# HGRN mixer, first head pair: decay tables in PSUM in place of SBUF

## Chip, cores and metric

One Trainium2 chip, one of its cores. The metric is the device time of one execution in microseconds (us). The kernel before takes 2683.29 us, the median of 3 runs (2683.0 to 2686.62).

## What is computed

The reference is a hybrid encoder trunk of two layers over 512 tokens of width 1024, in fp32. The first layer's mixer joins an HGRN2 gated linear recurrence (4 heads of 128x128 state, in both directions) and a Mamba-2 mixer; a dense SwiGLU follows. The second layer has an S5 mixer and an expert SwiGLU. The change concerns the HGRN2 part only:

```python
def _hgrn2_one_direction(q, k, v, logf):
    ...
    bc = jnp.cumsum(chunks(logf), axis=3)
    ...
        diff = bi[:, :, :, None, :] - bi[:, :, None, :, :]
        decay = _masked_exp(mask, diff)
        scores = jnp.einsum('bhtsd,bhsd->bhts', decay * qi[:, :, :, None, :], ki)
        o = (jnp.einsum('bhts,bhsv->bhtv', scores, vi)
             + jnp.einsum('bhtd,bhdv->bhtv', qi * jnp.exp(bi), state))
    ...
```

The score of query t against key s is the sum over d of q[t,d] k[s,d] exp(b[t,d] - b[s,d]), with b the running sum of the log forget gates. The backward direction is the same on the flipped sequence.

## The kernel before

It is one program with an instruction list for each engine, written by hand, and semaphores between them. The order on an engine is the order of the code; no scheduler moves anything.

The scores of a head are built over 9 levels. At level l the 512 tokens fall into blocks of 2·2^l; the queries of one half of each block meet the keys of the other half. A boundary between the halves splits the decay into a factor for the query and one for the key, so a level is an elementwise scaling of q and k and a product of the two on TensorE. Heads go in pairs: `unit(u)` gives (head, level, side) for u = 0 to 35, and units 0 to 17 (PAIR_UNITS is 18) are the first pair, two heads by turns, level 0 to 8. For one unit:

- ScalarE (L2128 to L2149) writes two decay tables of 128x512 into a buffer of the unit: B, the exponential of the prefix sums (L2144), and A, that of the suffix sums (L2146). At level 0 A is a copy of k (L2148). The buffers A_ and B_ are three of each in SBUF, taken by turns (u % 3). Before unit u ScalarE waits, from u = 3 on, until TensorE has read unit u-3 (s_gram, L2140), and from level 1 on until GpSimd has updated the sums for this level and head (s_upd, L2143), which is its work of unit u-2.
- GpSimd (L1059 to L1079) waits for ScalarE's unit u (s_exp), then brings both sums of this head to the next level: "near" (L1076) adds the block edges to the suffix sums and "far" (L1079) to the prefix sums, both 128x512 in SBUF, in place. It does so for all units of a pair but the last two. Ahead of it stand a memset (L1060) and the sums of the two key tables, `ksum` (L1064, two instructions).
- VectorE (L2792 to L2813) waits for s_exp and multiplies in place: B by q (L2798) and, from level 1 on, A by k (L2801). Then it takes the scores of unit u-2 out of PSUM (`scores`: L2710 for the diagonal at level 0, L2723 to copy by a mask up to level 6, L2726 and L2729 above).
- TensorE (L1461 to L1490) waits for the two products (s_X), then multiplies A and B into one of PSUM's banks 0 to 2, taken by turns, which VectorE must have emptied. Each such bank use is a slot, numbered 0 to 21 in a pair. Between slots stand fills (`dense_fill`, L1434 to L1438): pieces of the input projections that don't depend on HGRN2, accumulated in banks 6 and 7 and taken out by ScalarE (L2122). `fills_after_slot` says how many have been done after a slot, 29·(v+1)/22 rounded down in the first pair, so one or two after each slot. One fill is two matmul records of 128x512.

```python
a_at, prefix, suffix = ab_at + 2 * T * (u % 3), lf_at + T * hd, rs_at + 2 * T * side
if l:
    act.wait_ge(s_upd, updates_before(hd, l))
act.activation(by_halves(a_at + T + hs, -hs, hs), by_halves(prefix + hs, D_STEP - hs, hs), ACT.Exp)
```

After the last unit of the first pair TensorE computes the outputs of its two heads (`hg_out`, L1407) into banks 3 and 4. Banks 3, 4 and 5 hold nothing else while the units of the first pair run; in the second pair the normalisation of the first pair's outputs uses them. SyncE moves tables of the S5 layer between DRAM buffers meanwhile (L916, L920), and then loads further projection weights when fills have used the old ones (L955).

Of the kernel before, what the change touches and what calls it, by code (L numbers as in the profile page):

```python
# [10 lines left out]
ALU = mybir.AluOpType  # L11
ACT = mybir.ActivationFunctionType
AX_X = mybir.AxisListType.X

P = 128
# [38 lines left out]
def build_program(nc, I, out):  # L54
    x, p_in = I["x"], I["p"]
    _, T, D = x.shape
# [25 lines left out]
    with ctx:  # L82
        def sem(name):
            return ctx.enter_context(nc.semaphore(name))
# [15 lines left out]
        psum = ctx.enter_context(nc.psum_tensor("psum", [P, 8, 512], F32))  # L100
# [126 lines left out]
        s_X = sem("scaled_qk_ready")  # L227
        s_upd = sem("prefix_updated")
        s_gram = sem("gram_done")
# [119 lines left out]
        qT = hga.take(4 * T).rearrange(v4, a=4)  # L349
# [17 lines left out]
        q_at, k_at, lf_at, D_STEP = base, base + 4 * T, base + 20 * T, 4 * T  # L367

        UNITS, SIDES = HEADS * LEVELS, 2
        PAIR_UNITS, PAIR_SLOTS = 2 * LEVELS, 2 * (LEVELS + 2)  # L370

        def unit(u):

            pair, l, side = u // PAIR_UNITS, u % PAIR_UNITS // 2, u % 2
            return 2 * pair + side, l, side
# [4 lines left out]
        def first_slot(u):  # L380
            hd, l, side = unit(u)
            return PAIR_SLOTS * (hd // 2) + (2 * side + 1 if l == 0 else 2 + 2 * l + (side if l < LEVELS - 1 else 2 * side))

        def last_slot(u):
            return first_slot(u) + (unit(u)[1] == LEVELS - 1)

        def out_unit(hd):
            return PAIR_UNITS * (hd // 2 + 1) - 2 + hd % 2

        def updates_before(hd, l):  # L390

            return 2 * (LEVELS - 1) * (hd // 2) + 2 * (l - 1) + hd % 2 + 1

        def blocks_of(hs):
            return [[2 * hs, T // (2 * hs)], [1, hs]] if hs > 1 else [[2, T // 2]]

        def by_halves(at, step, hs):

            return bass.AP(sbuf, at, [[words, P], [step, 2]] + blocks_of(hs))
# [810 lines left out]
        def _(pe):  # L1210
# [191 lines left out]
            def hg_out(hd):  # L1402
                pe.wait_ge(s_gdr, last_slot(out_unit(hd)) + 1)
                if hd >= 2:
                    pe.wait_ge(s_mix, hd - 1)
                for c in range(TC):
                    m = pe.matmul(psum[:, 3 + hd % 2, :], vtok[:, c, hd * P:(hd + 1) * P], S_main[hd % 2][:, c, :],  # L1407
                                  start=c == 0, stop=c == TC - 1)
                m.then_inc(s_o, 1)
# [542 lines left out]
        def _(act):  # L1952
# [154 lines left out]
            def hg_square(hd):  # L2107
                act.wait_ge(s_o, hd + 1)
                act.activation(mixT[:, hd, :], psum[:, 3 + hd % 2, :], ACT.Square).then_inc(s_osq, 1)

            def hg_rms(hd):
                act.wait_ge(s_oss, hd + 1)
                act.activation(mixT[:, hd, :], psum[:, 5, :], ACT.Sqrt, bias=eps, scale=1.0 / P).then_inc(s_orms, 1)

            def fill_drain(i):
                name, b = DENSE[i]
                act.wait_ge(s_grp, 4 * gidx[name] + b + 1)
                if (name, b) == ("xs", 0):
                    act.wait_ge(s_X, PAIR_UNITS)
                    act.wait_ge(s_upd, 2 * (LEVELS - 1))  # L2120
                out_ = zs[:, b, :] if name == "z" else raw[b + 4 * (name == "bc")]
                act.activation(out_, psum[:, 6 + i % 2, :], ACT.Copy).then_inc(s_drA, 1)  # L2122
# [6 lines left out]
            for u in range(UNITS):  # L2129
                hd, l, side = unit(u)  # L2130
                hs = 1 << l
                for i in range(len(DENSE)):
                    if i != DT_BLOCK and unit_after[i] + 3 == u:
                        fill_drain(i)
                if u in (PAIR_UNITS + 3, PAIR_UNITS + 4):
                    hg_square(u - PAIR_UNITS - 3)
                if u in (PAIR_UNITS + 6, PAIR_UNITS + 10):
                    hg_rms((u - PAIR_UNITS - 6) // 4)
                if u >= 3:
                    act.wait_ge(s_gram, last_slot(u - 3) + 1)  # L2140
                a_at, prefix, suffix = ab_at + 2 * T * (u % 3), lf_at + T * hd, rs_at + 2 * T * side
                if l:
                    act.wait_ge(s_upd, updates_before(hd, l))  # L2143
                act.activation(by_halves(a_at + T + hs, -hs, hs), by_halves(prefix + hs, D_STEP - hs, hs), ACT.Exp)  # L2144
                if l:
                    m = act.activation(by_halves(a_at, hs, hs), by_halves(suffix, T + hs, hs), ACT.Exp)  # L2146
                else:
                    m = act.activation(by_halves(a_at, hs, hs), by_halves(k_at + T * hd, D_STEP + hs, hs), ACT.Copy)  # L2148
                m.then_inc(s_exp, 1)  # L2149
# [74 lines left out]
            for j in range(FJ):  # L2224
                act.wait_ge(s_drD, cumD[gidx[f"fu{j}"]])
                n = down_tile0 - 2 + j if j < 2 else down_tile0 + 2 * (j - 2) + 1
# [237 lines left out]
        def _(dve):  # L2464
# [129 lines left out]
            for n, (k, m0, count) in enumerate(ROW_TABLES):  # L2594
                src, sign0, sign1 = SIGNS[k]
                for q, sign in enumerate((sign0, sign1)):
                    m = dve.tensor_scalar(rowt[:, n, 0:count, q, :], src[:, m0:m0 + count, :], float(sign), None, ALU.mult)
# [14 lines left out]
            for n, (k, m0, count) in enumerate(ROW_TABLES):  # L2612
# [6 lines left out]
                for d in range(2):  # L2619
# [4 lines left out]
                    if up:  # L2624
                        m = dve.tensor_copy(where, src)
                    else:
                        for q in range(count):
                            m = dve.tensor_copy(table[:, :, d, hi - q], bank[:, q, d, :])
# [84 lines left out]
            def scores(u):  # L2713

                hd, l, side = unit(u)
                if l == 0:
                    diag_scores(hd)
                for v in range(first_slot(u), last_slot(u) + 1):
                    dve.wait_ge(s_gram, v + 1)
                    dve.wait_ge(s_gdr, v)  # L2720
                    bank = psum[:, v % 3, :]
                    if l < 7:
                        m = dve.copy_predicated(S_diag[side], masks[:, l, :].unsqueeze(1).broadcast_to([P, TC, P]),  # L2723
                                                bank.rearrange("p (c t) -> p c t", c=TC))
                    elif l == 7:
                        m = dve.tensor_copy(S_next[side], bank.rearrange("p (i j t) -> p i j t", i=2, j=2))  # L2726
                    else:
                        d = v - first_slot(u)
                        m = dve.tensor_copy(S_main[side][:, 2 * d:2 * d + 2, (2 - 2 * d) * P:(4 - 2 * d) * P],  # L2729
                                            bank.rearrange("p (i t) -> p i t", i=2))  # L2730
                    m.then_inc(s_gdr, 1)

            def hg_finish(hd):

                rms = mixT[:, hd, :]
                dve.wait_ge(s_orms, hd + 1)
                chain.link(dve.reciprocal(rms, rms))
                chain.settle()
                chain.link(dve.tensor_tensor(rms, psum[:, 3 + hd % 2, :], rms, ALU.mult))
                chain.settle()  # L2740
                dve.scalar_tensor_tensor(out=rms, in0=rms, scalar=parT[:, 48 + hd:49 + hd], in1=gT[:, hd, :],
                                         op0=ALU.mult, op1=ALU.mult).then_inc(s_mix, 1)
# [49 lines left out]
            for u in range(UNITS):  # L2792
                hd, l, side = unit(u)
                hs = 1 << l
                A, B = A_[u % 3], B_[u % 3]
                a_at = ab_at + 2 * T * (u % 3)
                dve.wait_ge(s_exp, u + 1)
                m = dve.tensor_tensor(B, B, qT[:, hd, :], ALU.mult)  # L2798
                if l:
                    a = by_halves(a_at, hs, hs)  # L2800
                    m = dve.tensor_tensor(a, a, by_halves(k_at + T * hd, D_STEP + hs, hs), ALU.mult)  # L2801
                m.then_inc(s_X, 1)
                if u >= 2:
                    scores(u - 2)
                if u in (PAIR_UNITS + 8, PAIR_UNITS + 12):
                    hg_finish((u - PAIR_UNITS - 8) // 4)
                if u in conv_at:
                    convolve(convolved)
                    convolved += 1
                if u == unit_after[DT_BLOCK] + 2:  # L2810
                    dt_parts()
# [88 lines left out]
            for c in range(TC):  # L2900
                for g in range(GROUPS):
                    y = yst[:, c, g * 256:(g + 1) * 256]
                    m = dve.tensor_scalar(y, y, ssy[:, 2, 2 * c + g:2 * c + g + 1], None, ALU.mult)
# [323 lines left out]
            for k in range(2):  # L3227
                for c in range(TC):
                    chain.link(dve.tensor_scalar(moe_hotR[:, k, c, :], rowi, rsel[:, k, c:c + 1], None, ALU.is_equal))
                    m = dve.tensor_scalar(moe_hotB[:, k, c, :], rowi[:, 0:SLOTC], bsel[:, k, c:c + 1], parti[:, c:c + 1],  # L3230
                                          ALU.is_equal, ALU.mult)
# [131 lines left out]
            for c in range(TC):  # L3363
                dve.wait_ge(s_yg[c], 32)
                for k in range(2):
                    m = dve.scalar_tensor_tensor(out=h[:, c, :], in0=yg[k][:, c, :], scalar=gate[:, k, c:c + 1],
                                                 in1=h[:, c, :], op0=ALU.mult, op1=ALU.add)
# [35 lines left out]
```

## Time and profile before

| what | value |
|---|---|
| runs before, median (lowest to highest) | 2683.29 us (2683.0 to 2686.62) |
| the profiled execution: its own time | 2682.27 us |
| its span in the trace | 2680.3 us |
| mean granted TensorE clock | 0.964 of full |
| busy: TensorE matmul | 2497.8 us (93%) |
| busy: VectorE / ScalarE / GpSimd | 1709.6 / 1259.5 / 233.4 us |
| the units of the first head pair | about 240 to 298 us of the span |

The span counts from the first to the last instruction of the execution. In rows, PE is the matmul side of TensorE and PEld its weight load, DVE is VectorE, ACT ScalarE, POOL GpSimd, SP SyncE; L1076 is line 1076 of the kernel before. The place names `stages` and `kept` are parts of SBUF; `psum` is PSUM. "PEclk" is the clock granted to TensorE as a share of 2.4 GHz, so 0.50 is 1.2 GHz. An engine's idle time costs something only where the work that it holds up is on the path to the end.

### The profile page before, as it was taken

How to read it: one execution, taken by the hardware profiler on the slowest of the kernel's cores; microseconds unless marked ns; L12 is line 12 of the kernel's file. 1: busy time of each engine (PE TensorE's matmuls, PEld its weight loads, DVE VectorE, ACT ScalarE, POOL GpSimd, SP SyncE). 2: the span in 40 equal slices, each digit the busy share in tenths (PEclk: the TensorE clock that was granted, in tenths of full speed). 3: DMA queues.
4: the chain of work that ended last, by engine and by line, in shares of the span. 5: the costliest groups of instructions: out<-in, count | busy, mean ns of one | idle time of the engine just before them, and what ended most of it. 6: DMA issues, size and time to landing. Idle time of an engine off the chain costs nothing.

```text
span 2680.3 us, 31498 instructions
## 1 busy us (share of the span) xinstructions
PE 2497.8 (93%) x12526; PEld 1999.5 (75%) x12526; DVE 1709.6 (64%) x2032; ACT 1259.5 (47%) x1419; POOL 233.4 (9%) x240
## 2 busy tenths in 40 slices
PE   7898988999998999869979999999999999999978
PEld 4444564478887887768769988998889988998853
DVE  6897788442223225593366688667876688667862
ACT  3433423132222223553245577566765577566741
POOL 4004735100000000000000000000000000000010
PEclk9999989999999999889779999999999999999989
DMA  6556410152223222534177799778997799777950
GB/s 165 174 177 185 108 63 32 49 179 95 94 94 102 95 94 77 186 120 149 40 255 252 252 348 366 268 243 285 375 317 244 253 346 368 268 252 267 371 213 32
DMA packets 316386, 526.14 MB, mean 196 GB/s; under 512 B 19286, under 2 KB 175546, under 8 KB 313578
## 3 DMA queue, kind: packets, MB, share of 16 engines
q1 hardware_dynamic: 287162, 479.73, 52.0%
q0 software_dynamic: 5888, 25.78, 3.1%
q10 hardware_dynamic: 23184, 18.55, 2.1%
q8 instruction: 102, 1.67, 0.2%
q14 instruction: 50, 0.41, 0.0%
HBM read 494.46 MB, written 45.81 MB: 202 GB/s over the span
## 4 chain that ended last, share of the span: by engine, by line
PE 81%; DVE 11%; ACT 2%; issue 2%; POOL 2%; DMA 1%; ACTq 0%; POOLq 0%; DVEq 0%
PE psum L1800 27%; PE psum L1368 16%; PE psum L1859 12%; PE psum L1633 5%; PE psum L1861 5%; PE psum L1257 4%; PE psum L1280 4%; PE psum L1438 1%; POOL stages L1076 1%; POOL stages L1079 1%; DVE stages L834 1%; DVE stages L844 1%; DVE stages L839 1%; DVE stages L835 1%; PE psum L1338 1%
## 5 line engine op out<-in xcount | busy, mean ns | idle before, releaser
L3261 DVE TENSOR_TENSOR stages_r<-kept,stages_r 128x2048 fp32r<-128x2048 f32 x336 | 769.2, 2291 | 242.5 <-ACT stages_r L2348 241.6
L2348 ACT ACTIVATE stages_r<-kept 128x2048 fp32r<-128x2048 f32 x336 | 637.4, 1912 | 228.5 <-PE psum L1800 104.2
L1800 PE MATMUL psum<-stages_r 128*128 128x512 f32 x3136 | 738.8, 393 | 3.2 <-issue 3.2
L1800 PEld LDWEIGHTS psum<-stages_r 128*128 128x128 f32 x3136 | 583.7, 188 | 127.0 <-issue 4.8
L1859 PE MATMUL psum<-stages_r 128*128 128x320 f32 x1792 | 464.7, 345 | 6.3 <-issue 3.2
L1368 PE MATMUL psum<-stages_r 128*128 128x512 f32 x1920 | 437.5, 390 | 3.2 <-ACT stages_r L1971 2.7
L1861 PE MATMUL psum<-stages_r 128*128 128x160 f32 x1792 | 423.1, 236 | 0.0
L1368 PEld LDWEIGHTS psum<-stages_r 128*128 128x128 f32 x1920 | 359.9, 188 | 79.6 <-ACT stages_r L1971 3.1
L1861 PEld LDWEIGHTS psum<-stages_r 128*128 128x128 f32 x1792 | 342.8, 191 | 2.0
L2920 DVE TENSOR_TENSOR stages_r<-kept,stages_r 128x2048 fp32r<-128x2048 f32 x54 | 123.8, 2292 | 345.2 <-ACT stages_r L2209 345.2
L1859 PEld LDWEIGHTS psum<-stages_r 128*128 128x128 f32 x1792 | 337.0, 188 | 9.0 <-DVE stages_r L3261 3.8
L2209 ACT ACTIVATE stages_r<-kept 128x2048 fp32r<-128x2048 f32 x54 | 103.5, 1917 | 334.6 <-PE psum L1368 220.8
L1633 PE MATMUL psum<-stages_r,stages_front_r 128*128 128x512 f32 x672 | 155.4, 394 | 6.8 <-DVE stages_front_r L2946 6.8
L1633 PEld LDWEIGHTS psum<-stages_r,stages_front_r 128*128 128x128 f32 x672 | 128.1, 191 | 34.1 <-issue 7.2
L1280 PE MATMUL psum<-stages,kept 128*128 128x512 f32 x256 | 118.5, 609 | 0.0
L1257 PE MATMUL psum<-kept,stages 128*128 128x512 f32 x256 | 111.5, 597 | 1.6 <-ACT stages L1976 0.8
L2384 ACT ACTIVATE stages<-stages 128x160 f32<-128x160 f32 x112 | 37.8, 338 | 158.3 <-DVE stages L3293 158.3
L1257 PEld LDWEIGHTS psum<-kept,stages 128*128 128x128 f32 x256 | 48.8, 192 | 62.4 <-issue 60.3
L1160 POOL DMA_INDIRECT stages<-moe_rows_by_token,stages x8 | 12.3, 1538 | 889.2 <-PE psum L1808 521.4
L1280 PEld LDWEIGHTS psum<-stages,kept 128*128 128x128 f32 x256 | 47.0, 192 | 54.1 <-issue 54.1
L3296 DVE TENSOR_TENSOR kept<-stages 128x160 f32<-128x160 f32 x112 | 36.6, 327 | 45.2 <-ACT stages L2384 45.2
L2144 ACT ACTIVATE stages<-stages 128x512 f32<-128x512 f32 x36 | 23.1, 642 | 81.0 <-PE psum L1477 37.8
(402 smaller groups left out, 2499.1 us busy)
## 6 DMA issues: line engine op xcount, KB each, us to landing
kept<-in_moe_w_gu_dram SPq DMA_DIRECT2D x224, 1024.0 KB, 6.5
kept<-in_moe_w_down_dram SPq DMA_DIRECT2D x112, 1024.0 KB, 6.5
kept<-in_ffn_w_gu_dram SPq DMA_DIRECT2D x28, 1024.0 KB, 5.1
kept<-in_ev_w_in_dram SPq DMA_DIRECT2D x16, 1024.0 KB, 6.2
kept<-in_ffn_w_down_dram SPq DMA_DIRECT2D x14, 1024.0 KB, 5.1
s_output_maps_by_state<-stages ACTq DMA_DIRECT2D x64, 128.0 KB, 2.0
s_input_maps<-stages ACTq DMA_DIRECT2D x32, 256.0 KB, 2.5
s_output_maps<-s_output_maps_by_state SPq DMA_DIRECT2D x32, 256.0 KB, 4.8
```

The source lines that it names most:

```text
L1257: m = pe.matmul(psum[:, b0 + b, 0:width], act[:, 4 * kk + k, b * P:(b + 1) * P], w[:, k, 0:width], **at)
L1280: m = pe.matmul(psum[:, b, :], *pair, start=kk == 0 and k == 0, stop=kk == 1 and k == 3)
L1368: m = pe.matmul(psum[:, 4 * (g % 2) + b, :], *pair, start=kk == 0 and k == 0 and n == 0, stop=kk == 1 and k == 3 and n == 2, skip_group_ch ...
L1633: m = pe.matmul(psum[:, 2 * c + hf, :], a[:, k, at], w[hf][:, k, :], start=j == 0 and k == 0 and n == 0, stop=j == FJ - 1 and k == 3 and n ...
L1800: m = pe.matmul(out_, a, b, start=start and n == 0, stop=stop and n == len(pairs) - 1, skip_group_check=True)
L1859: pe.matmul(bank[:, 0:2 * CAP], wh[:, k, fs], x_[:, k, :], start=k == 0, stop=False, skip_group_check=True)
L1861: m = pe.matmul(bank[:, 0:CAP], wl[:, k, fs], x_[:, k, 0:CAP], start=False, stop=k == 7, skip_group_check=True)
L2209: act.activation(f_high[t % 2], ring[:, n % RING, :].rearrange("p (k n) -> p k n", k=4), ACT.Copy).then_inc(s_wh, 1)
L2348: act.activation(w_high[n % WSLOTS], unit_tile(n), ACT.Copy).then_inc(s_wh, 1)
L2384: act.activation(lsil[fb], gate_up[fb][:, 0, :], ACT.Silu).then_inc(s_sil, 1)
L2920: dve.tensor_tensor(f_low[t % 2], ring[:, (SPLIT_RUNS[run][1] + t) % RING, :].rearrange("p (k n) -> p k n", k=4), f_high[t % 2], ALU.subtr ...
L3261: dve.tensor_tensor(w_low[n % WSLOTS], unit_tile(n), w_high[n % WSLOTS], ALU.subtract).then_inc(s_ws, 1)
```

## The change

In the first head pair ScalarE writes its exponentials to PSUM banks 3, 4 and 5, by turns, and VectorE reads them there and writes the products to the same SBUF buffers as before. Table B of unit u has number 2u-2 and table A number 2u-1 (units 0 and 1 have only B, numbers 0 and 1, and A stays a copy in SBUF); number n lies in bank 3 + n % 3. The second pair (units 18 to 35) is as before.

The waits move with the writer of the SBUF buffers: in the first pair it is now VectorE that waits for s_gram of unit u-3. ScalarE no longer does, and waits for a free bank in its place: before table B of unit u for the products of unit u-2 (s_X at u-1), and before table A for the products of unit u-1 (s_X at u). No instruction is added, dropped or put in another place on any engine.

```diff
+        def decay_order(u):
+
+            return (u, None) if u < 2 else (2 * u - 2, 2 * u - 1)
+
+        def decay_bank(n):
+            return psum[:, 3 + n % 3, :]
+
+        def bank_halves(n, at, step, hs):
+
+            return bass.AP(psum, (3 + n % 3) * T + at, [[8 * T, P], [step, 2]] + blocks_of(hs))
+
...
-                if u >= 3:
+                if u >= PAIR_UNITS:
                     act.wait_ge(s_gram, last_slot(u - 3) + 1)
                 a_at, prefix, suffix = ab_at + 2 * T * (u % 3), lf_at + T * hd, rs_at + 2 * T * side
                 if l:
                     act.wait_ge(s_upd, updates_before(hd, l))
-                act.activation(by_halves(a_at + T + hs, -hs, hs), by_halves(prefix + hs, D_STEP - hs, hs), ACT.Exp)
-                if l:
+                nb, na = decay_order(u) if u < PAIR_UNITS else (None, None)
+                if nb is not None and nb >= 3:
+                    act.wait_ge(s_X, u - 1)
+                to_b = by_halves(a_at + T + hs, -hs, hs) if nb is None else bank_halves(nb, hs, -hs, hs)
+                act.activation(to_b, by_halves(prefix + hs, D_STEP - hs, hs), ACT.Exp)
+                if na is not None:
+                    if na >= 3:
+                        act.wait_ge(s_X, u)
+                    m = act.activation(bank_halves(na, 0, hs, hs), by_halves(suffix, T + hs, hs), ACT.Exp)
+                elif l:
                     m = act.activation(by_halves(a_at, hs, hs), by_halves(suffix, T + hs, hs), ACT.Exp)
                 else:
                     m = act.activation(by_halves(a_at, hs, hs), by_halves(k_at + T * hd, D_STEP + hs, hs), ACT.Copy)
                 m.then_inc(s_exp, 1)
...
                 dve.wait_ge(s_exp, u + 1)
-                m = dve.tensor_tensor(B, B, qT[:, hd, :], ALU.mult)
+                nb, na = decay_order(u) if u < PAIR_UNITS else (None, None)
+                if nb is not None and u >= 3:
+                    dve.wait_ge(s_gram, last_slot(u - 3) + 1)
+                m = dve.tensor_tensor(B, B if nb is None else decay_bank(nb), qT[:, hd, :], ALU.mult)
                 if l:
                     a = by_halves(a_at, hs, hs)
-                    m = dve.tensor_tensor(a, a, by_halves(k_at + T * hd, D_STEP + hs, hs), ALU.mult)
+                    from_a = a if na is None else bank_halves(na, 0, hs, hs)
+                    m = dve.tensor_tensor(a, from_a, by_halves(k_at + T * hd, D_STEP + hs, hs), ALU.mult)
                 m.then_inc(s_X, 1)
```

## Rows read from the trace of the kernel before

**Rows 1.** The page: the chain that ended last, share of the span by engine.
```profile
PE 81%; DVE 11%; ACT 2%; issue 2%; POOL 2%; DMA 1%; ACTq 0%; POOLq 0%; DVEq 0%
```

**Rows 2.** Stretches: length, busy time (instructions) by engine, PEclk, DMA share, GB/s.
```profile
240.00:298.00 58.00, 43.82 (x200) 26.75 (x201) 50.31 (x53) 24.36 (x41) 55.24 (x37) 0.95 0.81 218
298.00:345.00 47.00, 47.00 (x176) 26.87 (x175) 29.26 (x31) 20.31 (x31) 33.05 (x22) 1.00 0.14 46
...
370.00:375.00 5.00, 4.12 (x20) 4.02 (x20) 4.96 (x6) 0.83 (x2) 2.58 (x2) 0.50 0.00 0
```

**Rows 3.** Waits, 240 to 298 us: waiter <- releaser, us in total, times, longest.
```profile
ACT stages L2144 <- POOL stages L1079: 32.4, 16, 4.3
```

**Rows 4.** Timeline of POOL: start us, us, engine, line, what, [idle before <- releaser].
```profile
241.97 2.96 POOL L1064 TENSOR_TENSOR kept<-stages 128x512 f32<-128x512 f32 x2
244.88 1.94 POOL L1076 TENSOR_TENSOR stages<-stages 128x512 f32<-128x512 f32 x1
...
250.82 1.96 POOL L1076 TENSOR_TENSOR stages<-stages 128x512 f32<-128x512 f32 x1
...
290.10 1.38 POOL L1079 TENSOR_TENSOR stages<-stages 128x512 f32<-128x512 f32 x1
291.44 1.49 POOL L1076 TENSOR_TENSOR stages<-stages 128x512 f32<-128x512 f32 x1
293.01 1.38 POOL L1079 TENSOR_TENSOR stages<-stages 128x512 f32<-128x512 f32 x1
```

**Rows 5.** Timeline of DVE: behind unit 2, second product of unit 16, unit 17.
```profile
251.32 0.68 DVE L2710 TENSOR_TENSOR stages<-psum,kept 128x512 f32<-128x512 f32 x1
...
293.41 1.53 DVE L2801 TENSOR_TENSOR stages<-stages 128x512 f32<-128x512 f32 x1
...
295.66 0.69 DVE L2798 TENSOR_TENSOR stages<-stages 128x512 f32<-128x512 f32 x1
296.27 0.68 DVE L2801 TENSOR_TENSOR stages<-stages 128x512 f32<-128x512 f32 x1
```

**Rows 6.** Timeline of POOL, instructions that meet no product of two SBUF tables.
```profile
303.51 1.51 POOL L1076 TENSOR_TENSOR stages<-stages 128x512 f32<-128x512 f32 x1
...
351.41 1.07 POOL L1079 TENSOR_TENSOR stages<-stages 128x512 f32<-128x512 f32 x1
...
366.24 1.05 POOL L1076 TENSOR_TENSOR stages<-stages 128x512 f32<-128x512 f32 x1 [1.56 <-ACT stages L2146]
367.36 1.05 POOL L1079 TENSOR_TENSOR stages<-stages 128x512 f32<-128x512 f32 x1
```

**Rows 7.** Timeline of DVE: a product of a PSUM table beside 351.41 of rows 6.
```profile
351.70 0.69 DVE L2739 TENSOR_TENSOR stages<-psum,stages 128x512 f32<-128x512 f32 x1
```

**Rows 8.** Timeline of ACT: unit 16, and one table read from PSUM.
```profile
291.57 0.63 ACT L2144 ACTIVATE stages<-stages 128x512 f32<-128x512 f32 x1 [1.76 <-POOL stages L1079]
292.11 0.61 ACT L2146 ACTIVATE stages<-stages 128x512 f32<-128x512 f32 x1
...
299.89 0.58 ACT L2122 ACTIVATE stages<-psum 128x512 f32<-128x512 f32 x1
```

**Rows 9.** Timeline of PE: slots 3, 4 and 18.
```profile
252.15 1.13 PE L1477 MATMUL psum<-stages 128*128 128x128 f32 x8 [1.83 <-DVE stages L2710]
...
254.84 1.05 PE L1477 MATMUL psum<-stages 128*128 128x128 f32 x8
255.73 1.02 PE L1436 MATMUL psum<-kept,stages 128*128 128x512 f32 x2
256.59 1.05 PE L1477 MATMUL psum<-stages 128*128 128x128 f32 x8
...
294.99 1.13 PE L1490 MATMUL psum<-stages 128*128 128x256 f32 x4 [0.89 <-DVE stages L2801]
```

**Rows 10.** Timeline of SP: the last table moves, and the weights after them.
```profile
267.71 22.04 SPq L920 DMA_DIRECT2D s_toeplitz<-s_kernels  x32
303.04 7.24 SPq L955 DMA_DIRECT2D kept<-in_ev_w_in_dram  x2
```

## The prediction

> **What bounds the kernel now.** I read the page first. The chain that ended last lies on TensorE for 81% of the span [rows 1], so a change pays where TensorE waits, and only there. The second view is the table of stretches [rows 2]. Over the first head pair, 240 to 298 us, TensorE is busy for 43.82 of 58 us and GpSimd for 55.24, with VectorE at 50.31; in the 47 us behind it TensorE is busy for 47.00. So the first pair is a hole in TensorE's work, and what is gained there arrives at a TensorE that is never idle for the next 47 us. The third view, the waits of that stretch, names the holder: ScalarE waits 16 times and 32.4 us in total for GpSimd's far update [rows 3]. The fourth, the timeline of GpSimd, shows it without a gap: unit 2's near update starts at 250.82 and unit 15's far update ends at 293.01 + 1.38 = 294.39, with no idle time noted in between [rows 4]. That is 43.57 us for 14 units, 3.11 us each.
>
> **Why GpSimd is slow there.** The same updates have two durations. At level 7 near takes 1.49 us and far 1.38 [rows 4]; with no product of two SBUF tables beside them they take 1.05 and 1.05 [rows 6]. At level 0 near takes 1.94 in the first pair [rows 4] and 1.51 alone [rows 6]. VectorE's products have two durations too: the product of A and k takes 1.53 us beside GpSimd and 0.68 for unit 17, when GpSimd is through [rows 5]. The starts fit an exchange of turns: the product that starts at 293.41 ends at 294.94, 0.55 us behind the end of GpSimd's update at 294.39. Each waits for the other's whole instruction. The deciding question is whether a product of one PSUM and one SBUF table does so as well. L2739 is of that kind, starts at 351.70 and takes 0.69 us [rows 7], while GpSimd's far update from 351.41 to 352.48 takes 1.07 [rows 6], its time alone. L2710 reads PSUM and SBUF at 251.32, inside the near update that runs from 250.82 to 252.78, and takes 0.68 [rows 4, 5]. Neither pays anything.
>
> **The change part by part.**
>
> *GpSimd's updates.* Nothing is removed, but in the first pair VectorE has no product of two SBUF tables left beside them: 18 of B and 16 of A now read PSUM. Per unit of level 1 to 7 the saving is (1.49 - 1.05) + (1.38 - 1.05) = 0.77 us. I take level 7's figure for all, since near at level 0 gives 1.94 - 1.51 = 0.43, the same as 0.44 at level 7. For units 2 to 14 that is 13 x 0.77 = 10.0 us. Unit 0's near gives 0.43 and unit 1's far, which also met a product, 0.33. The two key sums take 2.96 us with unit 0's and unit 1's products beside them [rows 4]; alone they can't be seen, they lie between 2.96 (nothing gained) and 2 x 1.07 = 2.14. I take 2.16, nearer the second since they too are contiguous 128x512 sums, so 0.8. GpSimd's update of unit 14 then ends 10.0 + 0.43 + 0.33 + 0.8 = 11.6 us earlier.
>
> *The last link.* Slot 18 needs unit 16, which needs the update of unit 14. Now that takes from 290.10 + 1.38 = 291.48 [rows 4] to 294.99 [rows 9], 3.51 us. Afterwards it is 0.09 to wake ScalarE, 292.11 - 291.57 = 0.54 for table B and 0.61 for table A [rows 8], 0.05, then 296.27 - 295.66 = 0.61 and 0.68 for two products that wait for nobody [rows 5], and 0.05: 2.63 us. That gives 0.9 more, and slot 18 starts 11.6 + 0.9 = 12.5 us earlier, at 282.5.
>
> *ScalarE's tables in PSUM.* The trace has no table written to PSUM. The nearest rows are 0.61 to 0.63 us from SBUF to SBUF and 0.58 from PSUM to SBUF [rows 8]. I take 0.61. From below, it can save 0.03 a table and that changes nothing; from above no row limits it, so the point from which it decides counts. ScalarE's table A of unit u now waits for the products of unit u-1, which makes a new circle: table A 0.61, wake 0.05, two products 0.61 + 0.68, wake 0.07, together 2.02 us a unit. GpSimd alone needs 1.05 + 1.05 + 0.1 = 2.2 us at level 7 and more below, so the circle is covered until table A costs 0.8 us. The cover is thin, 0.18 us a unit.
>
> *VectorE.* A product from PSUM is priced at 0.69 [rows 7]. VectorE's unit was 3.11 us; now it is two products and one taking of scores, 0.61 + 0.61 + 0.8, about 2.0 us, under GpSimd's 2.2. Its new wait for TensorE's unit u-3 costs nothing: its own previous step, the scores of unit u-3, has waited for the same slot. The Trainium skill, "VectorE: DVE Perf Modes", section on the TRN2 errata, speaks against the change: it gives a VectorE instruction with a PSUM source 120 fixed cycles, and one with an SBUF source 58, at 0.96 GHz. By that the 32 products that follow an update would cost 65 ns more each, the circle would be 2.15 us in place of 2.02, still under 2.2, and the sum would lose 0.13 us, in the last link. The trace doesn't agree: 0.69 from PSUM, 0.68 from SBUF.
>
> *TensorE.* It must not become the bound. A slot costs it 255.73 - 254.84 = 0.89 us and a fill 256.59 - 255.73 = 0.86 [rows 9]. From slot 3 to slot 18 there are 15 slots and 20 fills (5 are done after slot 3, 23 after slot 17, and 3 before it), 13.4 + 17.2 = 30.6 us. Slot 3 waited 1.83 us until 252.15 for L2710 [rows 9], which stands behind unit 2's products; these come 2.0 us earlier (0.8 + 0.43 from GpSimd, 0.84 from the shorter second product), so slot 3 follows its own fills at 252.15 - 1.83 = 250.3. TensorE could then be at slot 18 at 280.9, 1.6 us ahead of its data: no bound, but the most that any further speed of the others could give.
>
> *What lies behind.* From slot 18 on everything hangs on TensorE or on this chain, and moves as a whole. SyncE has sent the last table move at 267.71 + 22.04 = 289.75 and then waits until 303.04 for the fills to free weights [rows 10]; 12.5 us earlier is 290.5, still behind 289.75, so the loads come earlier too. This margin of 0.8 us is thin but harmless, as those weights are used only late in the second pair. The second pair has nothing changed.
>
> The sum is 12.5 us. The profiled execution's own time is 2682.27 (span 2680.3), 1.0 below the median of the runs shown; it becomes 2669.8, and the median 2683.29 becomes **2670.8 us**. What a measurement of this kernel tells from no change is 0.2%, 5.4 us.
>
> **The rivals.**
>
> - *The circle is longer than GpSimd.* If ScalarE's table in PSUM costs 1.2 us, twice the rows, the circle is 2.61 us and each of 14 units gives 3.11 - 2.61 = 0.5: 7 us, 2676.3. For it: the margin of 0.18 us. Against: reading PSUM is no dearer for either engine. The same time would come if the products kept a part of the exchange.
> - *The change doesn't free the engines.* If it is the SBUF write of a product that stands in GpSimd's way, nothing moves: 2683.3. Against it stand rows 6 and 7; for it, that they are single meetings of 0.7 us each.
> - *The clock.* The second pair has a stretch at a granted clock of 0.50, 1.2 GHz, in which TensorE is busy for 4.12 of 5 us while VectorE is for 4.96 [rows 2]. The whole pair now comes 12.5 us earlier, and where the clock falls and rises may change. One such stretch at 2.4 GHz would save half of 4.12, 2.1 us; two more or two fewer are 4 us either way: 2666.8 or 2675.0.
> - *Slower.* The mechanism is the circle again, ScalarE's table A behind the products of the unit before. It decides against the change where it is longer than 3.11 us, that is, where a table in PSUM costs over 3.11 - 1.41 = 1.7 us. At 2.1 us the circle is 3.51, 14 x 0.4 = 5.6 us are lost, and the time is 2688.9. For it speaks only that no row shows such a write; against it, that it takes 3.4 times the row.
>
> **How the numbers follow.** The forecast has 0.70, the longer circle 0.09, no effect 0.05, the clock 0.12, slower 0.04. The forecast's own bounds: key sums that give nothing, 11.7 us; TensorE's 14.1 as the most; so 2669.2 to 2671.6, and 2 us more on either side for a clock that falls once more or less. The range for 8 in 10 takes in the clock's 2666.8 at one end and the longer circle's 2676.3 at the other: 2666.5 to 2677. Under 2677.9 is faster by over 0.2%: forecast, clock and half of the longer circle's cases, 0.86. Same: the rest of those and no effect, 0.10. Slower: 0.04.
>
> **What would show it.** GpSimd's near and far updates in the first pair at 1.05 to 1.1 us from level 5 on, VectorE's second product at 0.69 in place of 1.53, ScalarE's PSUM tables under 0.8, GpSimd still without idle time, and 12 to 13 us less between 240 us and slot 18, with the stretches behind unchanged in length. GpSimd waiting for ScalarE's table A, and ScalarE for L2801's successor, would mean the longer circle. GpSimd still at 1.49 and 1.38 would refute the whole. A right first pair with another total would put the difference on the clock rows of the second pair or later.

## The result, and the profile after

The changed kernel takes 2669.72 us, the median of 6 runs (2664.72 to 2669.97); the kernel before takes 2682.21 us in 6 runs beside them (2678.51 to 2686.62). The ratio is 0.9953 by the medians, given as 0.995 with a 95% interval of 0.9938 to 0.9963. So it is 12.5 us faster, and the interval lies beyond the 0.2% that counts as no change. The prediction was 2670.8 us, range 2666.5 to 2677.0.

The profiled execution after is the shortest of the six, 2664.72 us with a span of 2662.8; by its span the gain is 17.5 us where the medians say 12.5. The first pair explains 12.6 of them; the rest is taken up below. In the changed kernel near is L1087, far L1090, the key sums L1075, the memset L1071; the tables B and A are L2159 and L2163, their products L2820 and L2824; TensorE's slots are L1488, L1493 and L1501.

The stretch of the first pair after the change, columns as in [rows 2], and two of the waits between 240 and 290 us, as in [rows 3]:

```profile
240.00:285.00 45.00, 41.21 (x198) 27.07 (x199) 33.27 (x52) 23.91 (x41) 42.38 (x37) 0.93 0.92 252
```

```profile
ACT psum L2159 <- POOL stages L1090: 20.4, 16, 3.4
...
PE psum L1488 <- DVE stages L2824: 0.4, 2, 0.2
```

TensorE is busy for 41.2 of 45 us, where it was for 43.8 of 58, and GpSimd is still the one with no gap. VectorE's 53 instructions took 50.31 us, its 52 now take 33.27. ScalarE still waits for GpSimd, 20.4 us in place of 32.4; the 0.4 us that TensorE waits for products were 7.0.

GpSimd after, the counterparts of [rows 4]: key sums and unit 0, the first update of unit 2, and the last three updates.

```profile
241.92 2.51 POOL L1075 TENSOR_TENSOR kept<-stages 128x512 f32<-128x512 f32 x2
244.39 1.49 POOL L1087 TENSOR_TENSOR stages<-stages 128x512 f32<-128x512 f32 x1
...
249.55 1.51 POOL L1087 TENSOR_TENSOR stages<-stages 128x512 f32<-128x512 f32 x1
...
278.84 1.05 POOL L1090 TENSOR_TENSOR stages<-stages 128x512 f32<-128x512 f32 x1
279.85 1.05 POOL L1087 TENSOR_TENSOR stages<-stages 128x512 f32<-128x512 f32 x1
280.98 1.04 POOL L1090 TENSOR_TENSOR stages<-stages 128x512 f32<-128x512 f32 x1
```

Units 2 to 15 run from 249.55 to 282.02, 32.47 us in place of 43.57. VectorE and ScalarE at the end of the first pair, and slot 18 on TensorE (counterparts of [rows 5], [rows 8], [rows 9]):

```profile
281.08 0.69 DVE L2820 TENSOR_TENSOR stages<-psum,stages 128x512 f32<-128x512 f32 x1 [0.20 <-ACT psum L2163]
281.69 0.68 DVE L2824 TENSOR_TENSOR stages<-psum,stages 128x512 f32<-128x512 f32 x1
```

```profile
279.93 0.60 ACT L2159 ACTIVATE psum<-stages 128x512 f32<-128x512 f32 x1 [1.01 <-POOL stages L1090]
280.46 0.58 ACT L2163 ACTIVATE psum<-stages 128x512 f32<-128x512 f32 x1
```

```profile
250.31 1.13 PE L1488 MATMUL psum<-stages 128*128 128x128 f32 x8
...
282.42 1.13 PE L1501 MATMUL psum<-stages 128*128 128x256 f32 x4
```

Both products take 0.67 to 0.69 us in every unit, beside GpSimd's updates too. A table written to PSUM costs ScalarE 0.58 to 0.60 us from unit 4 on, where to SBUF it was 0.61 to 0.63 (0.62 to 0.65 before that, where it was 0.65 to 0.70). Slot 18 starts at 282.42; it was at 294.99.

### The profile page after: what moved, and what is told of

Its sections match the earlier page's. It is cut to its first block, busy times and chain, and to the rows that moved or that the text cites. A ratio compares the mean times of both kernels' runs of the same rounds, so it can differ in the third digit from the quotient of the medians.

```text
span 2662.8 us, 31513 instructions
## 1 busy us (share of the span) xinstructions
PE 2494.8 (94%) x12526; PEld 2001.4 (75%) x12526; DVE 1692.3 (64%) x2032; ACT 1259.1 (47%) x1419; POOL 223.6 (8%) x240
## 4 chain that ended last, share of the span: by engine, by line
PE 82%; DVE 10%; ACT 2%; issue 2%; POOL 2%; DMA 1%; ACTq 0%; POOLq 0%; DVEq 0%
PE psum L1811 27%; PE psum L1379 16%; PE psum L1870 12%; PE psum L1644 5%; PE psum L1872 5%; PE psum L1268 4%; PE psum L1291 4%; PE psum L1449 1%; PE psum L1349 1%; DVE stages L845 1%; DVE stages L855 1%; POOL stages L1087 1%; DVE stages L850 1%; DVE stages L2492 1%; DVE stages L846 1%
## 5 line engine op out<-in xcount | busy, mean ns | idle before, releaser
L1291 PE MATMUL psum<-stages,kept 128*128 128x512 f32 x256 | 118.5, 609 | 0.0
L1449 PE MATMUL psum<-stages,kept 128*128 128x512 f32 x128 | 60.4, 607 | 0.0
```

Source lines behind the costliest of these rows:

```text
L1291: m = pe.matmul(psum[:, b, :], *pair, start=kk == 0 and k == 0, stop=kk == 1 and k == 3)
L1449: m = pe.matmul(bank, w[:, k, b * P:(b + 1) * P], hnT[:, n, :], **at)
```

## The experiments

Since GpSimd's first memset starts between 240.15 and 242.28 us in the profiles, whatever the kernel, the runs are compared by the distance from that start to slot 18. Before it is 294.99 - 240.20 = 54.8 us, after 282.42 - 240.15 = 42.3.

| run | memset starts | slot 18 | distance | time, us |
|---|---|---|---|---|
| only table A in PSUM | 240.60 | 290.57 | 50.0 | 2675.21 (one run) |
| only table B in PSUM | 242.28 | 291.04 | 48.8 | 2675.42 (one run) |
| table A written twice | 240.29 | 286.82 | 46.5 | 2670.81 (one run) |
| table B written twice | 240.32 | 283.23 | 42.9 | 2668.09 (one run) |
| updates cut short | 240.41 | 282.31 | 41.9 | not comparable |
| the change, again | 241.79 | 284.07 | 42.3 | 2669.55 (5 runs) |
| key sums on VectorE | 240.29 | 280.91 | 40.6 | 2664.68 (5 runs) |
| late tables in PSUM | 241.80 | 284.10 | 42.3 | 2667.79 (5 runs) |
| both steps | 242.06 | 282.66 | 40.6 | 2665.64 (5 runs) |

The times of single runs are read for nothing, since six runs of the change alone spread over 5 us.

**One table alone in PSUM.** For the first, ScalarE and VectorE take `nb` as None, so B stays in SBUF; for the second the same with `na`. ScalarE gets its wait for s_gram back in both, and VectorE loses its own.

```diff
-                if u >= PAIR_UNITS:
+                if u >= 3:
                     act.wait_ge(s_gram, last_slot(u - 3) + 1)
...
-                nb, na = decay_order(u) if u < PAIR_UNITS else (None, None)
-                if nb is not None and nb >= 3:
-                    act.wait_ge(s_X, u - 1)
+                nb, na = (None, decay_order(u)[1]) if u < PAIR_UNITS else (None, None)
...
```

> Only table A goes through PSUM; table B and its product with q stay in SBUF. The time measured is where slot 18 starts (294.99 before, 282.42 after the change). Theory (each product of two SBUF tables and each GpSimd update exclude each other): one exchange a unit is left, GpSimd's far update keeps its 0.33 us over the time alone (1.38 at level 7) and near falls to 1.05, so slot 18 starts about 5 us later than after the change, at 287 to 288. Rival (only the long product of A and k, 1.53 us, disturbs): near and far both at 1.05, slot 18 at 282.4.

> Only table B goes through PSUM; table A and its product with k stay in SBUF. Theory (mutual exclusion): the product of A still waits for an update and is longer than 0.69 (about 1.1 to 1.5 us), one of the two updates of a unit keeps about 0.44 us, slot 18 at 288 to 290. Rival (only A disturbs): as before the change, near 1.49 and far 1.38, slot 18 at 294 to 295.

GpSimd with only A in PSUM, the far update of unit 14 and the near update of unit 15 (both of level 7), and VectorE's two products beside them:

```profile
285.74 1.05 POOL L1090 TENSOR_TENSOR stages<-stages 128x512 f32<-128x512 f32 x1
286.75 1.49 POOL L1087 TENSOR_TENSOR stages<-stages 128x512 f32<-128x512 f32 x1
```

```profile
286.02 1.31 DVE L2816 TENSOR_TENSOR stages<-stages 128x512 f32<-128x512 f32 x1
287.26 0.68 DVE L2820 TENSOR_TENSOR stages<-psum,stages 128x512 f32<-128x512 f32 x1
```

The same with only B in PSUM, and the near update of unit 14 ahead:

```profile
285.24 1.50 POOL L1087 TENSOR_TENSOR stages<-stages 128x512 f32<-128x512 f32 x1
286.81 1.05 POOL L1090 TENSOR_TENSOR stages<-stages 128x512 f32<-128x512 f32 x1
287.82 1.49 POOL L1087 TENSOR_TENSOR stages<-stages 128x512 f32<-128x512 f32 x1
```

```profile
286.54 0.69 DVE L2818 TENSOR_TENSOR stages<-psum,stages 128x512 f32<-128x512 f32 x1
287.15 1.25 DVE L2822 TENSOR_TENSOR stages<-stages 128x512 f32<-128x512 f32 x1
```

In each case the product that still has two SBUF tables is long (1.31, 1.25) and the other short, so it is neither the product of A nor the one of B that is special. One of GpSimd's two updates keeps about 0.45 us. With B in PSUM the pace is 287.82 - 285.24 = 2.58 us a unit; with both in PSUM it is 279.85 - 277.72 = 2.13, by the start of near in the same two units. One exchange thus costs 0.45 us a unit. The theory holds and its rival, that only A's product disturbs, falls in both runs.

The expectation for A alone missed three things. I named far as the update that stays long; up to level 2 it was, but from unit 7 on it is near, as VectorE's product falls elsewhere in a shorter unit. And I expected some 5 us where the distance grew by 50.0 - 42.3 = 7.7. The 0.33 that I took was the smaller of the two delays. The products of B at level 0 also hold up the key sums and unit 0's near again: 2.95 and 1.94 us, as before the change, in place of 2.51 and 1.49. And unit 16's product of B meets GpSimd's last update, so that the last link, from 285.74 + 1.05 = 286.79 to slot 18 at 290.57, is 3.8 us in place of 2.5. For B alone the growth is 6.5, in the range given once the late start of 242.28 is taken off.

**A table written twice.** The first writing signals on `s_ac`, so that the second starts when it has ended; every later wait for `s_ac` counts 16 more. For table B the same two lines stand ahead of the writing of B.

```diff
+                    act.activation(bank_halves(na, 0, hs, hs), by_halves(suffix, T + hs, hs), ACT.Exp).then_inc(s_ac, 1)
+                    act.wait_ge(s_ac, u - 1)
                     m = act.activation(bank_halves(na, 0, hs, hs), by_halves(suffix, T + hs, hs), ACT.Exp)
```

> Table A of units 2 to 17 is written twice, the second after the first has ended, 0.6 us more between the products of one unit and those of the next. Theory (GpSimd sets the pace and the circle of table A and products, 2.0 us, is just covered): the circle becomes 2.6 us, over GpSimd's 2.1 to 2.35 at levels 3 to 7, GpSimd waits for ScalarE there, slot 18 at 286.5 to 287.5. Rival (the circle is not closed, there is slack elsewhere): only the last link grows, slot 18 at 283.0.

> Table B of units 2 to 17 is written twice in the same way. It lies outside the circle (it waits for the products of unit u-2 only) and between GpSimd's update and table A. Theory: GpSimd stays without idle time, only the last link grows by 0.6 us, slot 18 at 283.0. Rival (ScalarE's own time counts in full): as with table A twice, slot 18 at 286.5 or later.

GpSimd with table A written twice, units 14 and 15 of the first pair:

```profile
280.34 1.05 POOL L1087 TENSOR_TENSOR stages<-stages 128x512 f32<-128x512 f32 x1 [0.40 <-ACT psum L2165]
281.47 1.05 POOL L1090 TENSOR_TENSOR stages<-stages 128x512 f32<-128x512 f32 x1
282.93 1.05 POOL L1087 TENSOR_TENSOR stages<-stages 128x512 f32<-128x512 f32 x1 [0.42 <-ACT psum L2165]
```

The unit is 282.93 - 280.34 = 2.59 us, GpSimd now waits for ScalarE, and slot 18 stands at 286.82. The same 0.6 us a unit at table B leaves GpSimd without a gap and moves slot 18 to 283.23, 0.6 us in distance: that is the last link alone. Both came as the theory had it: with the change the circle of table A and the two products is closed and stands just under GpSimd's pace. 0.6 us on one side of it cost 4.2 us, on the other only the last link.

**GpSimd's updates cut short.** The sums of levels 1 to 8 in the first two heads are left out.

```diff
                     near = by_halves(suffix, T + hs, hs)
+                    if pair == 0:
+                        t = sbuf[:, suffix:suffix + 8]
+                        chain.link(pool.tensor_tensor(t, t, sbuf[:, prefix:prefix + 8], ALU.add))
+                        chain.settle()
+                        t = sbuf[:, prefix + 8:prefix + 16]
+                        pool.tensor_tensor(t, t, sbuf[:, prefix:prefix + 8], ALU.add).then_inc(s_upd, 1)
+                        continue
```

> GpSimd's updates of the first pair are cut to 8 columns each, so that part of the computation (the sums of levels 1 to 8 in the first two heads) is left out and the time shows what stands behind GpSimd as the next bound. Theory: TensorE's own 15 slots and 20 fills from slot 3 (250.3) on are then the bound, slot 18 at 280.9, 1.5 us before the change's 282.4 and no earlier, and TensorE idle nowhere in between. Rival (the circle of table A and products, 2.0 us a unit, or VectorE's 2.0 us a unit is longer than TensorE's mean 2.04 a slot): slot 18 later than 281.5, with TensorE waiting for the products.

TensorE in this run, slots 3 and 18, and what GpSimd and ScalarE wait for between 240 and 285 us:

```profile
251.75 1.05 PE L1495 MATMUL psum<-stages 128*128 128x128 f32 x8
...
282.31 1.03 PE L1508 MATMUL psum<-stages 128*128 128x256 f32 x4
```

```profile
POOL stages L1089 <- ACT psum L2170: 24.5, 14, 3.3
ACT psum L2170 <- DVE stages L2831: 16.0, 15, 2.6
```

From slot 3 to slot 18 TensorE takes 282.31 - 251.75 = 30.56 us and waits for no product: the 30.6 us of its own work are right. But slot 18 is at 282.31, not 280.9, because slot 3 starts 1.4 us later than with the change (250.31). The last six matmuls of slot 1 start at 247.58 and still take 1.49 us here, where with the change the eight at 246.76 take 1.05. TensorE's clock rose later in this run: from 246 to 248 us it was granted 0.50, where with the change it was 0.84. So the next bound behind GpSimd is TensorE, as expected, and where it stands depends on when the clock rises; of the two outcomes, which the expectation had set apart by the time of slot 18 and by TensorE's waits, the time pointed to the wrong one and the waits to the right one. The execution as a whole took 2944.89 us: with these sums left out, other values reach the choice of experts, which may be why; I didn't look further, and read nothing from it.

**The change again, with three steps further.** Key sums on VectorE:

```diff
-                for hd in (2 * pair, 2 * pair + 1):
-                    if pair:
-                        pool.wait_ge(s_gram, diag_slot(hd - 2) + 1)
+                for hd in (2 * pair, 2 * pair + 1) if pair else ():
+                    pool.wait_ge(s_gram, diag_slot(hd - 2) + 1)
...
+            for hd in range(2):
+                dve.tensor_tensor(ksum[hd], kT[0][:, hd, :], kT[1][:, hd, :], ALU.add).then_inc(s_ks, 1)
```

Late tables (`LATE = (29, 31)`; ScalarE also waits there until banks 3 and 5 have been read):

```diff
+            if u in LATE:
+                return 0, 2
...
-                if u >= PAIR_UNITS:
+                if u >= PAIR_UNITS and u not in LATE:
                     act.wait_ge(s_gram, last_slot(u - 3) + 1)
...
+                if u in LATE:
+                    act.wait_ge(s_mix, 1)
+                    act.wait_ge(s_orms, 2)
```

> The change as it stands, timed on the same chip as the three variants below, and a second look at where its time lies. Expected: 12 to 13 us under the kernel before, slot 18 at 42.3 us behind the start of GpSimd's memset, and in the stretches behind it differences of up to 5 us that go with the granted clock alone (the first profile was 17.5 us shorter than that of before, the median 12.5).

> VectorE, idle until 242.6 us, computes the two key sums of the first pair in place of GpSimd (2.51 us there). Theory (GpSimd's chain sets the first pair from its memset on): near of unit 0 starts 2.5 us earlier, slot 18 at 39.8 us behind the memset, 2667.2 where the change has 2669.7. Rival (TensorE's own work, 30.6 us from slot 3 to 18, takes over as the bound): less than 1.6 us are gained.

> In the second pair banks 3 and 5 are free for tables from unit 29 on; the tables of units 29 and 31, whose products meet GpSimd there, go through PSUM. Theory (exclusion works the same there, and VectorE is the bound of that stretch): VectorE's products of unit 29 and 31 fall from 0.68 + 1.55 and 1.54 + 1.53 to 0.69 each, 2.5 us of VectorE time; TensorE waited 0.95 and 0.88 us for them, so 1 to 2 us less in all. Rival (TensorE, at the lower granted clock there, is the bound): no difference over 0.5 us.

> Key sums on VectorE and the late tables together. Theory: the two gains add up, 3.5 to 4.5 us under the change, about 2665.5. Rival: the granted clock's stretches shift and give back as much as 4 us of it.

Against the kernel before, 2679.51 us in 9 runs on this chip, the ratios are: the change 0.9959 (0.9945 to 0.9972), key sums 0.9944 (0.993 to 0.9958), late tables 0.9955 (0.9941 to 0.9968), both 0.9949 (0.9935 to 0.9962). The change again is 10.0 us under before here, by medians, where 12 to 13 were expected; its interval, 7.5 to 14.7 us, holds both. Slot 18 is where it was to 0.1 us in distance.

With the key sums moved, GpSimd's first update shows why only 42.3 - 40.6 = 1.7 us of the expected 2.5 came:

```profile
240.29 1.80 POOL L1071 MEMSET stages<- 128x2048 f32 x1 [1.23 <-issue]
242.82 1.53 POOL L1086 TENSOR_TENSOR stages<-stages 128x512 f32<-128x512 f32 x1 [0.73 <-ACT stages L2166]
```

It now waits 0.73 us for ScalarE's first unit, whose table load (1.28 us, from 240.16) was hidden behind the key sums before. TensorE did not take over as the bound, as the rival had it: slot 3 starts at 249.06 and 30.6 us from there are 279.7, 1.2 us ahead of slot 18. The run medians, 2664.68 against 2669.55, differ by 4.9 us, more than these 1.7. In the two profiles (spans 2662.8 and 2667.6, 4.8 us apart) 1.5 us lie ahead of the memset and 1.7 up to slot 18, and 1.6 behind. What lies ahead of the memset is not from the step, whose first instruction starts at 240.18; TensorE's granted clock from 60 to 90 us was 0.94 here and 0.89 in the change again. What lies behind slot 18 can't be put down to the step either way. The runs don't overlap (2663.49 to 2666.99 against 2667.54 to 2669.87), so the variant was the faster one here, but only 1.7 us of it are followed to their cause.

The late tables did what they should on the products themselves: those of units 29 and 31 take 0.68 us each (351.62, 352.22, 360.01 and 360.62). But TensorE's waits between 333 and 388 us did not change:

```profile
PE psum L1492 <- DVE stages L2831: 6.3, 3, 3.7
```

They are 6.3 us in 3 times in the change again too (between 333 and 390 us). VectorE's timeline says why. With the late tables, from the four convolution steps ahead of unit 29 on:

```profile
346.55 5.15 DVE L2785 SCALAR_TENSOR_TENSOR stages<-stages,kept 128x510 f32<-128x510 f32 x4
351.62 0.68 DVE L2827 TENSOR_TENSOR stages<-psum,stages 128x512 f32<-128x512 f32 x1
352.22 0.68 DVE L2831 TENSOR_TENSOR stages<-psum,stages 128x512 f32<-128x512 f32 x1
```

And in the change again:

```profile
346.31 4.46 DVE L2778 SCALAR_TENSOR_TENSOR stages<-stages,kept 128x510 f32<-128x510 f32 x4
350.69 0.69 DVE L2820 TENSOR_TENSOR stages<-stages 128x512 f32<-128x512 f32 x1
351.29 1.55 DVE L2824 TENSOR_TENSOR stages<-stages 128x512 f32<-128x512 f32 x1
```

The product of unit 29 gains 0.87 us, but ends at 352.90 where it ended at 352.84. ScalarE no longer waits for TensorE before unit 29, so GpSimd's updates of units 29 and 30 start at 344.77 and 347.41 in place of 346.85 and 351.04, and stand beside more of the convolution steps, which read two SBUF operands each; these took 0.7 us more. The meeting has moved, it is not gone. Unit 31 had no meeting left to remove: its products took 0.69 and 0.68 us in the change again, and the 1.54 and 1.53 of the expectation were those of the kernel before. The medians, 2667.79 and 2669.55, are 1.8 us apart, with runs from 2666.25 to 2670.13: not told apart. So no difference came, as the rival said, but for another reason than TensorE's low clock. Whether TensorE (granted 0.70 over 341 to 381 us in both) would have used up a gain of VectorE's stays open.

Both steps together are no better than the first alone (2665.64 and 2664.68). Their 3.9 us under the change lie in the range expected of them, but by luck: the first step moved slot 18 by 1.7 us in distance and not by 2.5, and the second gave nothing.

## Why the prediction was right

*GpSimd sets the pace, and the exchange with VectorE's products is what slows it.* Right. Unit 14's far update ended at 279.89, 11.6 us earlier, as worked out. Two of its terms were off and made up for each other. The key sums gave 2.96 - 2.51 = 0.45 us, not 0.8: alone they take 1.25 us each, not the 1.07 of an update. The 13 units gave more than 13 x 0.77, since level 1 saves more than level 7: far at level 1 went from 1.47 to 1.04, 0.43 where level 7 has 0.33. That the sum came out at 11.6 is luck in these two terms. The start of near in unit 2 went from 250.82 to 249.55, 1.27 us, and the 13 units from there to 279.89 gained 291.48 - 250.82 - (279.89 - 249.55) = 10.3 where 10.0 were expected.

*A product with one PSUM table stands in nobody's way.* Right, by all 34 of them (0.67 to 0.69 us) and by the two runs with one table each. The rival that it is a product's SBUF write that stands in GpSimd's way is out: the products still write SBUF, and GpSimd's updates are short. The two single meetings in the trace of before were enough.

*ScalarE's table at 0.61, circle 2.02.* A table in PSUM takes 0.58 to 0.65, 0.58 to 0.60 from unit 4 on. The circle was covered, and thinly: the run with table A written twice, about 2.6 us round, is what the first rival described, and it costs 4.2 us in distance; the fourth is the same circle made longer. Both failed on the price of a PSUM table alone.

*The last link* was 282.42 - 279.89 = 2.53 us, against 2.63.

*VectorE's price from PSUM.* 0.67 to 0.69 us in every unit, as from SBUF when nothing interferes (0.69 and 0.68, [rows 5]). The dearer PSUM source that the Trainium skill's page "VectorE: DVE Perf Modes" gives in its section on the TRN2 errata is not seen in these products.

*TensorE's 30.6 us* are confirmed to 0.1 by the run with short updates. The margin of 1.6 us was 1.5: slot 3 at 250.31 and 30.6 give 280.9, slot 18 came at 282.42.

*The clock.* This rival was the only one to show, and as one execution against another, not as a change of the median. Of the profiled execution's 17.5 us, 12.6 are there at slot 18, and the outputs of the second head pair (L1407, now L1418) stand 13.2 us earlier (the last matmul moved from 409.2 to 396.0). A stretch after it differs in little but the clock. Before:

```profile
475.00:485.00 10.00, 4.68 (x24) 4.19 (x24) 9.09 (x12) 1.82 (x8) 1.49 (x2) 0.67 0.14 52
485.00:495.00 10.00, 10.00 (x27) 5.47 (x27) 5.16 (x13) 4.29 (x7) 0.00 (x0) 0.82 0.00 1
```

And 13 us earlier, after the change:

```profile
462.00:472.00 10.00, 4.68 (x24) 4.19 (x22) 8.82 (x12) 1.82 (x8) 1.23 (x2) 0.66 0.17 52
472.00:482.00 10.00, 10.00 (x31) 4.98 (x30) 5.16 (x13) 4.29 (x7) 0.00 (x0) 1.00 0.00 1
```

TensorE had been busy for less than half of the first ten us in both. In the next ten it got 0.82 of the clock before and all of it after, and did 31 matmul records in place of 27. Behind it the lead is 15.0 us (first matmul of L1606, now L1617, from 501.5 to 486.5). The next large step comes near 1310 us, where the granted clock differs again (0.55 from 1310 to 1322 us before, 0.79 from 1294.4 to 1306.4 after): the first of the 64 matmuls of L1772, now L1783, starts at 1314.4 and 1298.6, a lead of 15.8 us, and the last at 1327.8 and 1309.5, a lead of 18.3, of which 17.5 are left at the end. In the change's second profile the stretch from 475 to 485 us stands at 0.75; its lead is 10.9 us at slot 18 and 9.3 at L1617 (492.2), and that execution's time is 2669.55. So the 5 us are not shown to be a gain of the change: two executions of the same code differ by as much, and such steps go either way. The medians leave 12.5 us in the first measurement and 10.0 in the second. What is shown to 0.1 us is the 12.5 in distance to slot 18 (54.8 - 42.3); that the first difference of medians agrees with the forecast as closely is luck.

## What to carry to other kernels

Where two engines are both without a gap and the same instruction has two durations, look for what runs beside it in each case: the short one is the price alone, and the difference counts once for each meeting. In this kernel one operand moved to PSUM was enough to end the meeting of a VectorE product with GpSimd; it needs free banks, and the waits for these banks close a new circle, whose length against the pace decides. Then check what the next engine can still follow: here the gain ends 1.5 us further on, at TensorE's own work. Check too what the freed engine will meet next: in the second pair the same step let GpSimd start earlier, into other VectorE instructions with two SBUF operands, and gave nothing.

## What the runs showed that I had not expected

One of the two exchanges left in place costs GpSimd 0.45 us a unit at level 7 whichever of VectorE's two products causes it, while both together cost 0.78 (a pace of 291.44 - 288.53 = 2.91 us against 2.13): two meetings cost less than twice one. And the start of the whole stage, GpSimd's first memset, wanders from 240.15 to 242.28 us between executions whose code is alike up to there. In the profiles where it starts behind 241.7, TensorE's granted clock from 60 to 90 us was 0.89, in those where it starts at 240.1 to 240.6 it was 0.94. So a profile's absolute times can't be compared below 2 us; distances from a common instruction agree to 0.1 (42.27, 42.28 and 42.30 in the three profiles in which the change's first pair is the same).
